# GLA heads 1 to 3 by pairs of strips in seven block products, weight sums by accumulating DMAs

## What is computed

```python
proj = rmsnorm(h, norm_g) @ w_in            # 528 x 1024 @ 1024 x (1024 q + 1024 k + 2048 v + 16 gate + 2048 r)
log_a = log_sigmoid(g_low @ w_gate_up + b_gate) / 16
q = q * 256 ** -0.5
# per head, in chunks: b = cumsum(log_a); o = causal(q e^b (k e^-b)^T) v + (q e^b) S; S = e^b_last S + (k e^(b_last-b))^T v
o = rmsnorm(o, head_norm_g)
h = h + (o * silu(r)) @ w_out
```

## Time and profile before

| | |
|---|---|
| median of the runs | 1004.57 us |
| span of the profiled execution | 1002.4 us |
| all that the profile gives of this execution's own time is its span; median less span | 2.2 us |
| TensorE busy | 994.3 us, 99% |
| VectorE busy | 732.4 us, 73% |
| ScalarE busy | 552.2 us, 55% |
| GpSimd busy | 90.6 us |
| DMA | 107.69 MB, 107 GB/s on average |

### The profile page before, as it was taken

How to read it: one execution, slowest core, us unless ns; L and a number is a source line. 1 busy time by engine, 2 the same in 40 slices (tenths; PEclk the granted TensorE clock), 3 DMA queues, 4 the chain that set the end, 5 groups by cost and what they waited for, 6 DMA issues and landing times.

```text
span 1002.4 us, 19364 instructions
## 1 busy us (share of the span) xinstructions
PE 994.3 (99%) x7843; PEld 940.7 (94%) x7843; DVE 732.4 (73%) x1190; ACT 552.2 (55%) x915; POOL 90.6 (9%) x97
## 2 busy tenths in 40 slices
PE   9999999999999999999999999999999999999998
PEld 8999999999999999998889989999899989988897
DVE  6874677477567875435889976898589966989875
ACT  6754654564465554334566655656366645566633
POOL 0000000000000000000232211222112211210000
PEclk9999999999999999999999999999999999999999
DMA  8221231132122113333334432444244533486332
GB/s 293 78 71 64 67 101 45 63 103 68 64 72 97 44 63 127 105 108 104 113 82 122 108 137 60 134 103 137 89 114 110 120 117 91 124 257 233 115 106 84
DMA packets 42392, 107.69 MB, mean 107 GB/s; under 512 B 4784, under 2 KB 12848, under 8 KB 42304
## 3 DMA queue, kind: packets, MB, share of 16 engines
q1 hardware_dynamic: 41584, 105.78, 34.6%
q10 hardware_dynamic: 720, 0.68, 0.2%
HBM read 98.34 MB, written 7.90 MB: 106 GB/s over the span
## 4 chain that ended last, share of the span: by engine, by line
PE 89%; DVE 6%; ACT 2%; issue 2%; DMA 0%; DVEq 0%; ACTq 0%
PE psum L2076 50%; PE psum L2452 13%; PE psum L2371 7%; PE psum L2430 3%; PE psum L2566 3%; PE psum L2201 2%; DVE w_lo L1226 1%; PE psum L2411 1%; PE psum L2149 1%; PE psum L2573 1%; PE psum L2197 1%; PE psum L2399 1%; PE psum L2398 1%; PE psum L2400 1%; PE psum L2170 1%
## 5 line engine op out<-in xcount | busy, mean ns | idle before, releaser
L1226 DVE TENSOR_TENSOR w_lo<-raw,w_hi 128x1024 fp32r<-128x1024 f32 x156 | 191.5, 1242 | 38.3 <-ACT w_hi L682 28.0
L682 ACT ACTIVATE w_hi<-raw 128x1024 fp32r<-128x1024 f32 x156 | 162.9, 1052 | 47.8 <-PE psum L2371 29.5
L2076 PE MATMUL psum<-xh,w_hi 128*128 128x264 f32 x768 | 159.1, 288 | 0.2 <-DVE w_lo L1240 0.2
L2076 PE MATMUL psum<-xl,w_hi 128*128 128x264 f32 x768 | 155.9, 285 | 0.0
L2076 PE MATMUL psum<-xh,w_lo 128*128 128x264 f32 x768 | 155.2, 283 | 0.0
L2076 PEld LDWEIGHTS psum<-xh,w_hi 128*128 128x128 f32 x768 | 118.6, 189 | 1.6 <-issue 1.4
L2076 PEld LDWEIGHTS psum<-xl,w_hi 128*128 128x128 f32 x768 | 119.5, 188 | 0.0
L2076 PEld LDWEIGHTS psum<-xh,w_lo 128*128 128x128 f32 x768 | 119.1, 189 | 0.0
L624 POOL TENSOR_TENSOR sub<-sub,cst 128x128 f32<-128x128 f32 x64 | 50.8, 796 | 650.1 <-DMA sub<-sums 649.8
L2076 PE MATMUL psum<-y_lo,w_hi 128*128 128x264 f32 (+2 forms) x336 | 79.6, 299 | 0.0
L2452 PE MATMUL psum<-y_lo,w_hi 128*128 128x256 f32 x312 | 57.9, 287 | 0.1
(11 more groups left out here) (353 smaller groups left out, 2486.5 us busy)
## 6 DMA issues: line engine op xcount, KB each, us to landing
raw<-w_all SPq DMA_DIRECT2D x143, 512.0 KB, 3.5
sub<-sums SPq DMA_DIRECT2D x16, 264.0 KB, 7.2
y_keep<-sq SPq DMA_DIRECT2D x14, 256.0 KB, 2.2
y<-y_keep SPq DMA_DIRECT2D x14, 256.0 KB, 6.5
sub<-sums SPq DMA_DIRECT2D x16, 200.0 KB, 6.3
yr<-y_keep SPq DMA_DIRECT2D x12, 256.0 KB, 4.9
sub<-sums SPq DMA_DIRECT2D x16, 136.0 KB, 4.9
hT<-xT SPq DMA_DIRECT2D x8, 264.0 KB, 5.3
```

The source lines that it names most:

```text
L682: nc.scalar.activation(w_hi[:, n % HI_RING, :], raw[:, n % LO_RING, :], ACT.Copy).then_inc(hi_made, 1)
L1226: nc.vector.tensor_tensor(w_lo[:, n % LO_RING, :], raw[:, n % LO_RING, :], w_hi[:, n % HI_RING, :].bitcast(F32), ALU.subtract).then_inc(lo ...
L2076: i = nc.tensor.matmul(o, w[a][:, k % KT, :], x[b][:, k, c0:c1], start=k == first and a == b == 0, stop=k == last and a == 1)
```

## The change

Head 0 keeps its strips. For heads 1 to 3 the 12 strips become six pairs, 18 in all: q (Q0, Q1), k (K0, K1), v (V1, V0), r (R1, R0), w (V3, V2), s (R3, R2). A pair is a 2 x 2 block product (weights: two strips by two halves of the inner dimension; tokens: two halves of 264) and is computed from seven products of 4 k-tiles x 3 parts = 12 matmuls of 264 columns (`gp`). Products 1, 6 and 7 add up in one PSUM bank; ScalarE copies that bank out after each (`keep`), VectorE adds or subtracts the other products (`pair_out`, four of 264 columns a pair). The products stand in the order 1, 3 of the pair before, 2, 6, 5, 7, 4.

The weight sums s1, s2, s3, s4 of a pair are made by DMAs: SP loads one term of each, GpSimd issues an accumulating DMA for the other. The chunks of a pair are a (loaded), e (s2 and s4, not loaded as a whole), b (loaded, s3 added to its first half).

The tokens are normed once on VectorE (`norm_tokens`), in place in hT; then token sums, high parts on ScalarE and low parts on VectorE are made for the seven products, over the place of xh, xl and in new tiles. hT is loaded again before the output projection is added. The factor of q goes into the head norm's eps for all heads. Values of heads 1 to 3 need no root, so their split is two instructions instead of five. The gate's low-rank input takes the root, so `gate_read` is gone. All lists of calls are rewritten.

```diff
+GP = [(x, h) for h in range(1, GLA_HEADS) for x in "qkvrws"]
+GP_STRIPS = {"q": ("Q", 0, 1), "k": ("K", 0, 1), "v": ("V", 1, 0), "r": ("R", 1, 0), "w": ("V", 3, 2), "s": ("R", 3, 2)}
+GP_BANK = {1: 2, 6: 2, 7: 2, 2: 3, 5: 0, 3: 0, 4: 1}
```

SP, the loads of pair n:

```diff
+                if x == "a":
+                    load(m)
+                elif x == "b":
+                    a = w_all[AT[f"p{n:02d}a"]]
+                    s2, s4 = pair_raw(n, "e")
+                    if n == 1:
+                        sp.wait_ge(strip_made, 8)
+                        sp.wait_ge(xn_made, KT)
+                    elif n:
+                        sp.wait_ge(prod_done, GP_AT[(5, n - 2)])
+                    if n:
+                        sp.wait_ge(s1_sum, 16 * n)
+                    sp.dma_start(gs1(n)[0], w_all[AT[f"p{n:02d}b"], :, 0:CH // 2]).then_inc(s1_loaded, 16)
...
+                        sp.wait_ge(prod_done, GP_AT[(6, n - 2)])
+                    if n:
+                        sp.wait_ge(s2_sum, 16 * n)
+                    sp.dma_start(s2, a[:, 0:CH // 2]).then_inc(s2_loaded, 16)
+                    load(m)
+                    if n >= 2:
+                        wait_chunk_used(sp, m - 1 - LO_RING)
+                    if n:
+                        sp.wait_ge(s4_sum, 16 * n)
+                    sp.dma_start(s4, a[:, CH // 2:CH]).then_inc(s4_loaded, 16)
...
+                if n == CHUNK["W2b"]:
+                    sp.wait_ge(prod_done, len(GP_ORDER))
+                    for d in range(KT):
+                        sp.dma_start(hT[:, d, :], xT[:, d, :]).then_inc(h_loaded[d], 16)
```

GpSimd, the sums of pair n:

```diff
+                pool.wait_ge(s1_loaded, 16 * (n + 1))
+                pool.dma_start(s1_, from_b[:, CH // 2:CH], accum_op=ALU.add).then_inc(s1_sum, 16)
+                pool.wait_ge(s2_loaded, 16 * (n + 1))
+                pool.wait_ge(s1_sum, 16 * (n + 1))
+                pool.dma_start(s2, s1_, accum_op=ALU.add).then_inc(s2_sum, 16)
+                pool.wait_ge(w_loaded[b % LO_RING], 16 * LOADS[b])
+                if n:
+                    pool.wait_ge(s3_sum, 16 * n)
+                pool.dma_start(s3, from_a[:, 0:CH // 2], accum_op=ALU.add).then_inc(s3_sum, 16)
+                pool.wait_ge(s4_loaded, 16 * (n + 1))
+                pool.wait_ge(s2_sum, 16 * (n + 1))
+                pool.dma_start(s4, s2, accum_op=ALU.add).then_inc(s4_sum, 16)
```

ScalarE:

```diff
+            def keep(n, i):
+                act.wait_ge(prod_done, GP_AT[((1, 6, 7)[i], n)])
+                if n:
+                    act.wait_ge(out_made, gp_out_at(n - 1, ("11", "12", "21")[i]))
+                nc.scalar.activation((u1, u2, u3[:])[i], bank(GP_BANK[1], 0, HALF), ACT.Copy, scale=(1.0, 1.0, -1.0)[i]).then_inc(copied, 1)
```

ScalarE, end of head 0:

```diff
+                    token_sums_high(1)
+                    gla_value(0, 3)
+                    pair_high(0, "e")
+                    act.wait_ge(xn_made, KT)
+                    done(act, "R03")
+                    tokens_high(0, 0)
+                    gla_square(0, 2)
+                    gla_values_hi(0, 3)
+                    tokens_high(1, 0)
...
+                    s1_high(0)
+                    gla_gate(0, 3)
+                    tokens_high(1, 1)
+                    token_sums_high(3)
```

VectorE, start of head 1:

```diff
+                    pair_out(n, "11")
+                    first_low(n + 1)
+                    gla_out(h - 1, 3)
+                    head_add(h - 1, 3)
+                    if h == 1:
+                        gate_sum(h, 0)
+                        gate_sum(h, 1)
+                        difs_first(h)
+                        difs_second(h)
+                    pair_out(n, "22")
+                    pair_out(n, "21")
```

VectorE, pair r:

```diff
+                    mul_qj(h)
+                    half_inverse(h - 1, 0)
+                    n = pair("r", h)
+                    pair_out(n - 1, "12")
+                    pair_low(n, "b")
+                    pair_out(n, "11")
+                    half_inverse(h - 1, 1)
+                    mul_qc(h)
+                    gla_values_lo(h, 0)
+                    muls_far(h)
+                    muls_k(h)
+                    first_low(n + 1)
+                    pair_out(n, "22")
+                    pair_out(n, "21")
+                    pair_low(n + 1, "a")
+                    pair_low(n + 1, "e")
+                    s1_low(n + 1)
```

TensorE:

```diff
+            def gp(product, n):
+                w = pair_weights(n, product)
...
+                if product == 1:
+                    if n:
+                        pe.wait_ge(copied, 3 * n)
...
+                elif product == 6:
+                    pe.wait_ge(copied, 3 * n + 1)
+                elif product == 7:
+                    pe.wait_ge(copied, 3 * n + 2)
+                elif product == 3:
+                    pe.wait_ge(out_made, gp_out_at(n, "22"))
+                elif n:
+                    pe.wait_ge(out_made, gp_out_at(n - 1, {2: "11", 5: "12", 4: "21"}[product]))
+                x = GP_X[product]
+                o = bank(GP_BANK[product], 0, HALF)
+                for k in range(KT // 2):
+                    for a, b in PARTS:
+                        i = nc.tensor.matmul(o, w[k][a], x[b][:, k, :], start=product not in (3, 6, 7) and k == a == b == 0,
...
-                strip(f"R{h}0", x1)
-                gla_transposed(h, 0)
-                strip(f"V{h}1", x1)
-                strip(f"R{h}1", x1)
...
+                    for x in "kvr":
+                        n = pair(x, h)
+                        gp(1, n)
+                        gp(3, n - 1)
+                        if x == "k":
+                            head_sum(h - 1)
+                        gp(2, n)
+                        gp(6, n)
+                        if x == "r":
+                            gla_transposed(h, 0)
+                        gp(5, n)
+                        gp(7, n)
+                        gp(4, n)
+                gla_scores(h)
```

More of the change, by code:

```diff
@@ L261, in program @@
         acc = sb("acc", [P, T])
-        rstd = sb("rstd", [P, T])
+        with ExitStack() as one:
+            rstd = sb("rstd", [P, T], F32, one)
+        rstd_lo = sb("rstd_lo", [P, T], F32R)
         rtok = sb("rtok", [P, NBLK + 1])
@@ new lines, in _ @@
+                n = pair("w", h)
+                keep(n, 0)
+                gla_scores_hi(h)
+                gla_gate(h, 1)
+                pair_high(n, "b")
+                pair_high(n + 1, "a")
+                keep(n, 1)
+                s1_high(n + 1)
+                if h + 1 < GLA_HEADS:
+                    gate_abs(h + 1, 0)
+                keep(n, 2)
+                if h + 1 < GLA_HEADS:
+                    gate_abs(h + 1, 1)
+                pair_high(n + 1, "e")
+                if h + 1 < GLA_HEADS:
+                    gate_exp(h + 1)
+                else:
+                    y_high(0)
@@ L1447, in y_low, with first_low, s1_low @@
                     tt(y_lo[:, i, :], y[:, i, :], y_hi[:, i, :].bitcast(F32), ALU.subtract, ylo_made)
+            def first_low(n):
+                if n == len(GP):
+                    split(CHUNK["W0a"])
+                    return
+                dve.wait_ge(hi_made, CHUNK[f"p{n:02d}a"] + 1)
+                m = CHUNK[f"p{n:02d}a"]
+                tt(w_lo[:, m % LO_RING, 0:CH // 2], raw[:, m % LO_RING, 0:CH // 2], w_hi[:, m % HI_RING, 0:CH // 2].bitcast(F32), ALU.subtract, half_lo)
+            def s1_low(n):
+                if n == len(GP):
+                    return
+                dve.wait_ge(s1hi_made, n + 1)
+                dve.wait_ge(s2_sum, 16 * (n + 1))
+                raw_, low = gs1(n)
+                tt(two(low), two(raw_), gs1_hi.bitcast(F32), ALU.subtract, s1lo_made)
@@ new lines, in _ @@
+                    gla_mask(0)
+                    gla_scores_lo(0)
+                    ahead("V02")
+                    for k in range(KT // 2, KT - 1):
+                        norm_tokens(k)
+                    gate_min(1, 0)
+                    norm_tokens(KT - 1)
+                    gate_min(1, 1)
+                    token_sum(0)
+                    gla_out(0, 0)
+                    gla_values_lo(0, 1)
+                    token_sum(2)
+                    gla_gate(0, 2)
+                    token_sum(1)
@@ L1504, in _ @@
+                pair_low(n + 1, "a")
+                pair_low(n + 1, "e")
+                s1_low(n + 1)
+                if h + 1 == GLA_HEADS:
+                    y_low(0)
+                n = pair("s", h)
                 gla_out(h, 0)
                 gla_values_lo(h, 1)
-                ahead(f"R{h}2")
+                pair_out(n - 1, "12")
                 if h + 1 == GLA_HEADS:
-                    y_low(0)
-                gla_gate(h, 2)
+                    y_low(1)
+                else:
+                    gate_logs(h + 1)
+                    gate_sum(h + 1, 0)
@@ L1520, in _ @@
+            y_low(2)
+            gla_out(3, 3)
+            head_add(3, 3)
             head_sum_lo(3)
+            split(CHUNK["W1a"])
+            inverse("h3", acc[:])
             ahead("W0a")
-            y_low(2)
```

(23 more changed lines are left out.)

836 lines of the change are left out of this document (622 added, 214 removed).

## The result

The changed kernel takes 1029.24 us (median of two runs, 1028.31 to 1030.18) where the kernel before takes 1004.57: a ratio of 1.0248, 95% interval 1.0218 to 1.0278. It is slower; the forecast was 994 us, with a range of 980 to 1018. The profiled execution has a span of 1028.4 us.

A forecast was written before the change was run, and what follows sets the result against it. The prediction took TensorE's own queue to bound the kernel: 1004.6 less 26.3 us of matmuls, plus waits of 6 (steady heads), 8 (head 0's end) and 1 (the end), gives 993.3, stated as 994 us, range 980 to 1018.

The forecast's parts named there:

- TensorE's saving: Heads 1 to 3: twelve matmuls fewer in each of 18 pairs, 216 x 0.1217 = 26.3 us off TensorE's queue.
- X = 3.5 us: Weight sums: time of one 256 KB accumulating DMA, taken from a plain 512 KB load.
- It just fits.: Chain s1, s2, s4: s4 complete at -0.1 us from its pair's start, e's split wanted from about +0.1.
- rival C: Sum chain somewhat slow, X about 5: TensorE waits for e's low part, 20 us at most, 1007 us; chance 0.22.
- the walk: The engines' queues followed instruction by instruction with the assumed durations, to find where TensorE waits in heads 0 to 3.
- Rival D: GpSimd's queue makes a pair at least 2X, deciding from X = 6.6; at X = 8, 1030 us; chance 0.15.
- The steady head and the end: VectorE busy about 71 of 78.7 us a head; waits of 2 us a head, 1 us at the last head sum.
- The kb wait before the scores: Each head, pair r: VectorE's kb comes later than TensorE reaches the scores, 1.6 us of wait per head.
- Head 0's end: Passage from head 0 to head 1: TensorE waits for token norms, sums, high and low parts, about 8 us.
- output 22: Pair 0 at head 0's end: product 3 waits for this VectorE output behind the gate scans, 2.0 us lost.
- Sum: Whole kernel: 1004.6 less 26.3 saved, plus waits of 6, 8 and 1, gives 993.3 us, stated as 994.
- The DMA engines' share: Heads 1 to 3: 2.75 MB a pair, share 0.63, or 0.86 if accumulating bytes cost double; not full, but queues form.

The follow-up runs named there:

- experiment 1: The changed kernel without its 72 accumulating DMAs, each sum left as its one loaded term (wrong weights in heads 1 to 3): 1003.87 us, ratio 0.9991.
- experiment 14: The kernel before, plus plain and accumulating 256 KB DMAs by GpSimd into idle rows of y, singly and in threes: 1004.73 us (one run).
- Experiment 10: The changed kernel without the sums, VectorE's reciprocals and head norm of heads 0 to 2 cut to one column: 997.62 us, ratio 0.9930.
- Experiments 6 and 12: The changed kernel without sums, VectorE's and ScalarE's lists reordered: 1005.63 us; the same with reciprocals and head norm cut to one column: 998.32 us.
- experiment 11: The changed kernel with a third buffer for s1 and GpSimd's 72 DMAs as plain copies without addition: 1011.17 us, ratio 1.0061.
- experiment 13: The changed kernel without sums, plus 51 GpSimd DMAs (44 accumulating) into idle rows of y, almost nothing waiting for them: 1005.19 us, ratio 1.0007.

## Why the prediction was wrong

**TensorE's saving** (26.3 us): right. In undisturbed stretches the products run at the pace assumed (20.39 us for 168 matmuls in experiment 1, 0.1214 each).

**X = 3.5 us.** This step failed. I sized an accumulation of 256 KB by a plain load of twice the bytes. From DRAM by itself it takes 4.8 us to its landing (experiment 14); a link of the chain takes 4.95 on average here, and 5.33, 4.05 and 7.69 in the chain shown. The Trainium skill (DMA: Bandwidth & Descriptors, Anatomy of one DMA) led to an estimate of 2.6 or 3.2 us; this case's trace does not agree: even a plain one from DRAM, alone, took 3.1 to 3.8.

**"It just fits."** That the chain was the thing to watch, what starts it and what it ends in was right, and so was the sign of its failing (rival C: waits that end with w_lo of e, by ScalarE, by a DMA). C's X of about 5 is the mean that was measured. Its price was still too low, in three terms: the links scatter, and the late chains had 5.5 to 6.4; 1.6 us between landing and next issue over the chain's three links, which I had not counted; and 2 to 3 us of half clock behind each wait, which no row of before could show, since TensorE never stood still there. By an estimate with C's own sum, 3 x 5.85 (the mean of the late chains) + 1.6 - 10.6 = 8.6 us for s4, and TensorE waits 6.5 us, where 5.3 to 5.9 were measured. The three waits and their clock are 25 us, where C had at most 20. That one a head is waited for, in pair v, fits the walk, in which pairs v and r have nothing but bare products before them; that scores and attends let the chain catch up in the other pairs is argued, not shown by a run.

**Rival D** came nearest in time (1030 for 1029), by luck and not in cause: GpSimd's queue decides where X is over 6.6, and in this kernel X is 5, and in the chain shown each sum was issued 0.3 to 0.7 us after the DMA that it needed had landed. A pair takes 15.2 us by the distance of s1's issues, more than 2X.

**The steady head and the end** (71 of 78.7 us for VectorE, 2 us lost a head, 1 at the end): the work was sized right (70), the waits nearly so, and the clock behind them was left at nothing. Without sums, from scores to scores a head takes 83.9 and 82.3 us in place of 80.7, and from the last scores to the output projection 48.9 where it took 44.1, for the same number of matmuls. The kb wait before the scores is there, 1.95 us for my 1.6; behind one of the three the scores themselves last 1.7 longer, at half clock (152.50 to 155.90 above). The last head's attend waits 1.8, with 1.7 of half clock behind it, and its head sum 0.8. The rest is in waits of 0.2 to 0.5. Experiment 10 ties 6 us of it to the amount of VectorE's work: 15.2 us less give 6 back. Experiments 6 and 12 say that the order I tried instead gains nothing, with or without that work.

**Head 0's end** (8 us): about 9 in experiment 1 (53.5 us from 98.2, where TensorE begins to wait for the first quarter, to the first scores of head 1 at 151.7, less 39.3 of product matmuls, 3.1 of an attend, a head sum and transposes, and the 2.0 before the scores). Near in the sum, not in its terms: the first quarter 2.1 for 1.4, the second 1.2 for 1.5, output 22 2.4 for 2.0, keep(0,0) nothing for 2.7, and 26 matmuls at half clock around the first two waits, 2.8 us that I had not counted.

**Sum.** Forecast 993.3; beyond it without sums 10.6 (to 1003.9), the sums 25.4 (to 1029.2). The 15 us of waits in the forecast were about right without sums (15.4 measured above 0.18 us). Of the 10.6, 6.2 are TensorE at half clock, put at nothing; about 4 are not placed.

**The DMA engines' share** came near: 0.86 forecast if accumulating bytes cost double, 0.79 and 0.81 measured in heads 1 and 2. (The 2.75 MB of that sum are 2.88 in the units of the GB/s column.)

**Open.** How the 7 us between experiment 11 and experiment 1 divide between landing and the order of GpSimd's queue, and what part in X the other transfers have, is not settled; experiment 14 shows 4.8 us to the landing alone, experiment 13 has 6.3 in company. Why of the eight DMAs from SBUF in experiment 14 some took twice as long as others is open too. A version with less work on VectorE and the sums in time was not tried.

## What to carry to other kernels

Price a chain of dependent DMAs by its links: every link is a landing plus the issue behind it, and its sum is to be held against the time the buffers give, not against the bytes. A sum that comes out as just fitting, with the link's price taken from another kind of DMA, is a forecast of waits, and a wait costs its length and often half the clock behind it: count both. With VectorE busy 85% of the time only less work bought time; what was moved came back.

## What the runs showed of the hardware

An accumulating DMA of 256 KB issued by GpSimd from DRAM takes 4.8 us to its landing alone (3.4 without the addition), 0.87 us of GpSimd for 0.56, and more than twice the time of the DMA engines per byte (39.2% against 17.9% for 17.83 MB). A DMA share of 0.79 cost 1 to 2 us, not told apart from nothing, as long as nobody waited for it. GpSimd's additions made VectorE's two-operand instructions with SBUF operands 1.3 to 3.2 times as long (415 to 1317 ns).

After each wait of 5.3 to 5.9 us TensorE's matmuls ran at half clock for 4 to 6 us. Shorter waits went either way: half clock behind 2.1 us (at 100.3), 1.95 (at 151.7) and 1.8 (at 342.7) in experiment 1, full clock behind 2.4 (at 119.3) and two of 1.95 (at 235.6 and 317.8) in the same execution; in experiment 10 the 2.4 us wait at 119.7 did bring half clock. So by these rows the length of a single wait does not tell.
